# One table set for logarithm and exponential, evictions ahead of weight rounding on ScalarE, and a split order for the products of w2

## What is computed

```python
def first_block(x, p, ...):
    h = rms_norm(x, pre_norm_gain)
    q, k, v, z_a, b_gate, c_gate, u, z_c = split(h @ w_in, 8)      # 512 columns each
    attn = diff_attention(q, k, v, lam, slopes)                    # 4 heads, two softmaxes each
    attn = rms_norm(attn, subln_gain) * (1 - lambda_init) * silu(z_a)
    conv_out = b_gate * conv3(c_gate * u) * silu(z_c)
    x = x + rms_norm(concat(attn, conv_out) @ w_out, post_norm_gain)
    e = rms_norm(p @ w_ple_proj, ple_norm_gain)
    return x + sigmoid(x @ w_ple_gate) * e

def second_block(x, meta, ...):                                    # 16 meta tokens ahead
    n = rmsnorm(h, norm_mix)
    c_q, c_kv, k_pe, gq, gk, gv, ga, gg, gate_a, gate_b = split(n @ w_in)
    y_a = mla_branch(c_q, c_kv, k_pe, ...)                         # 8 heads, softmax
    y_b = gla_branch(gq, gk, gv, ga, gg, ...)                      # 4 heads with decay
    mix = sigmoid(gate_a) * (y_a @ w_o_mla) + sigmoid(gate_b) * (y_b @ w_o_gla)
    h = h + mix @ w_out
    h = h + peer_ffn(rmsnorm(h, norm_ffn), ...)                    # top 16 of 16384 experts
```

## Time and profile before

| | us |
|---|---|
| median of 3 runs | 2056.81 |
| lowest, highest | 2054.27, 2059.27 |
| the profiled execution | 2057.81 |
| its span, first to last instruction | 2056.0 |
| TensorE busy | 1908.5 |
| VectorE busy | 1288.2 |
| ScalarE busy | 1030.7 |
| GpSimd busy | 866.6 |
| mean granted clock of TensorE | 0.97 |

### The profile page before, as it was taken

How to read it: one execution, slowest core, us unless ns; L and a number is a source line. 1 busy time by engine, 2 the same in 40 slices (tenths; PEclk the granted TensorE clock), 3 DMA queues, 4 the chain that set the end, 5 groups by cost and what they waited for, 6 DMA issues and landing times.

```text
span 2056.0 us, 24907 instructions
## 1 busy us (share of the span) xinstructions
PE 1908.5 (93%) x9104; PEld 1484.3 (72%) x9104; DVE 1288.2 (63%) x2243; ACT 1030.7 (50%) x1656; POOL 866.6 (42%) x672
## 2 busy tenths in 40 slices
PE   7997989898978898998999989999998999999999
PEld 5775565467766666777777767777776888888887
DVE  6465374532336653468899968888863666656664
ACT  6465655744443426444444367777763433434341
POOL 5453452203122113775788789999983000000000
PEclk9999999999998899999999999999998999999999
DMA  6322223112111112442365547777679878888883
GB/s 223 116 103 103 103 92 98 43 31 92 42 62 42 42 41 82 143 161 90 98 225 196 187 160 236 264 273 284 255 263 373 301 281 296 286 287 294 283 297 138
DMA packets 98280, 359.15 MB, mean 175 GB/s; under 512 B 8480, under 2 KB 41504, under 8 KB 73328
## 3 DMA queue, kind: packets, MB, share of 16 engines
q1 hardware_dynamic: 98160, 357.56, 49.9%
HBM read 286.09 MB, written 71.30 MB: 174 GB/s over the span
## 4 chain that ended last, share of the span: by engine, by line
PE 55%; DVE 15%; POOL 14%; issue 7%; ACT 7%; DMA 2%; POOLq 0%; SPq 0%; ACTq 0%; DVEq 0%
PE ps L1434 11%; PE ps L1435 11%; PE ps L799 8%; PE ps L800 8%; POOL area L2651 6%; POOL wring_parts L2629 6%; PE ps L1245 3%; PE ps L788 2%; DVE area L2445 2%; ACT wring_parts L1479 2%; DVE area L2442 2%; PE ps L1221 1%; DVE area L2468 1%; PE ps L1382 1%; POOL wring_parts L2597 1%
## 5 line engine op out<-in xcount | busy, mean ns | idle before, releaser
L2597 POOL TENSOR_TENSOR wring_parts<-wring_parts,wring 128x512 fp32r<-128x512 f32 (+1 forms) x264 | 360.4, 1397 | 604.3 <-ACT wring_parts L1479 604.3
L1382 PE MATMUL ps<-sqbuf_parts,wring_parts 128*128 128x512 f32 x1024 | 410.3, 401 | 16.6 <-POOL wring_parts L2629 16.6
L1383 PE MATMUL ps<-normed_x_parts,wring_parts 128*128 128x512 f32 x1024 | 402.8, 393 | 0.0
L2629 POOL TENSOR_TENSOR wring_parts<-wring_parts,wring 128x512 fp32r<-128x512 f32 x256 | 328.3, 1314 | 66.8 <-ACT wring_parts L1884 63.8
L1382 PEld LDWEIGHTS ps<-sqbuf_parts,wring_parts 128*128 128x128 f32 x1024 | 194.7, 190 | 59.6 <-POOL wring_parts L2629 17.3
L800 PE MATMUL ps<-normed_x_parts,wring_parts 128*128 128x512 f32 (+1 forms) x624 | 235.5, 383 | 0.0
L1479 ACT ACTIVATE wring_parts<-wring 128x1024 fp32r<-128x1024 f32 (+1 forms) x132 | 125.3, 997 | 216.3 <-PE ps L800 181.3
L799 PE MATMUL ps<-resid_parts,wring_parts 128*128 128x512 f32 (+1 forms) x528 | 203.6, 393 | 26.3 <-issue 7.2
L1383 PEld LDWEIGHTS ps<-normed_x_parts,wring_parts 128*128 128x128 f32 x1024 | 194.7, 190 | 38.9
L1906 ACT ACTIVATE area<-ps 128x512 f32<-128x512 f32 x128 | 76.3, 597 | 195.1 <-PE ps L1383 195.1
L2531 DVE COPY area<-ps 128x512 f32<-128x512 f32 x128 | 138.8, 1086 | 54.2 <-PE ps L1409 54.2
(11 more groups left out here) (257 smaller groups left out, 3852.0 us busy)
## 6 DMA issues: line engine op xcount, KB each, us to landing
wring<-in_weights_dram SPq DMA_DIRECT2D x65, 1024.0 KB, 4.8
wring<-in_uT_dram SPq DMA_DIRECT2D x128, 512.0 KB, 4.3
area<-in_vT_dram SPq DMA_DIRECT2D x44, 1024.0 KB, 6.9
hidden_table<-area SPq DMA_DIRECT2D x32, 1024.0 KB, 6.5
gate_table<-area SPq DMA_DIRECT2D x32, 1024.0 KB, 8.1
area<-gate_table SPq DMA_DIRECT2D x32, 1024.0 KB, 9.1
wring<-in_vT_dram SPq DMA_DIRECT2D x20, 1024.0 KB, 7.2
rt<-hidden_table SPq DMA_DIRECT2D x32, 512.0 KB, 4.6
```

Source lines behind the costliest of these rows:

```text
L1382: pe.matmul(out, first[:, d], h_first[:, k, :], start=(k == 0), stop=False)
L1383: mm = pe.matmul(out, rest[:, d], h_rest[:, k, :], start=False, stop=(k == KD - 1))
L2597: ins = nc.gpsimd.tensor_tensor(rest[:, d, :], up[:, d, :], W(name)[:, d, :], ALU.subtract)
L2629: ins = nc.gpsimd.tensor_tensor(rest[:, a:a + PIECE], first[:, a:a + PIECE], u_raw[t % len(USLOT)][:, a:a + PIECE], ALU.subtract)
```

## The change

The table set that holds both Ln and Exp is loaded explicitly (`tables_for`), and explicit loads of the Silu, Sigmoid and Tanh sets stand ahead of the waits for the projections, with loads of the first set behind. ScalarE's order changes: q1's weights are rounded inside the rounding of h; in attention units `exps_a` and `exps_m` of u + 2 come ahead of the copy of the side projection, and `round_w` behind it; in a decay head the Tanh comes without `round_w` ahead, which moves to the end of the head; the four roots of the decay heads come ahead of the first Silu. On TensorE the products of w2 with inputs 6 and 7 are put behind others. On VectorE `scale_query(0)` moves from k == 6 to k == 3.

```diff
-            for m in range(4):
-                project_parts(("w2", m), MIX_PARTS, 3)
+            def mixed_out(m, a, ks):
+                key = ("w2", m)
+                if a == 0 and ks[0] == 0:
+                    claim(key)
+                up, low = split_arrived(f"w2{m}")
+                d = slice(a * P, (a + 1) * P)
+                for k in ks:
+                    if m == 0 and a == 0 and k % 2 == 0:
+                        pe.wait_ge(pair_split, 12 + k // 2 + 1)
+                    mm = two(pair(key)[:, a, :], (up[:, k, d], low[:, k, d]),
+                             (MIX_PARTS[0][:, k, :], MIX_PARTS[1][:, k, :]), k == 0, k == KD - 1)
+                if a == 1 and ks[-1] == KD - 1:
+                    fills(mm, key)
+            early, late = range(6), (6, 7)
+            for a in range(2):
+                mixed_out(0, a, early)
+            mixed_out(1, 0, early)
+            for a in range(2):
+                mixed_out(0, a, late)
+            mixed_out(1, 0, late)
+            mixed_out(1, 1, range(KD))
+            for m in (2, 3):
+                for a in range(2):
+                    mixed_out(m, a, range(KD))
...
+            def tables_for(name):
+                act.preload_act_table_set(name)
+            LOGS, SILUS, SIGMOIDS, TANHS = ("natural_log_exp_and_others", "silu_and_others", "sigmoid_and_others",
+                                            "exp_and_others")
...
+            tables_for(LOGS)
             for m in range(4):
                 act.wait_ge(x_first[m], 16)
...
-            round_h(0, "n1", T)
-            round_w(3)
+            round_h(0, "n1", T, {5: 3})
...
+                if u + 2 < len(UNITS_A):
+                    exps_a(u + 2)
                 if u in SIDE_A:
                     g, m = SIDE_A[u]
-                    round_w(SPLIT.index(f"{g}{m}") + NU)
+                    if g in ("zc", "za"):
+                        tables_for(SILUS)
...
-                if u + 2 < len(UNITS_A):
-                    exps_a(u + 2)
+                    round_w(SPLIT.index(f"{g}{m}") + NU)
+                    if g in ("zc", "za"):
+                        tables_for(LOGS)
...
             root("ple", T)
+            tables_for(SIGMOIDS)
             for m in range(4):
                 round_w(SPLIT.index(f"pg{m}") + NU)
                 copy_out(("pg", m), sgT[:, 2 * m:2 * m + 2, :], pair(("pg", m)), ACT.Sigmoid, scale=SCALE)
+                if m == 3:
+                    tables_for(LOGS)
...
+                if u + 2 < len(UNITS_M):
+                    exps_m(u + 2)
                 if u in SIDE_M:
...
                     elif g == "gk":
+                        copy_out(key, gk[:, m, :], flat(key)[:, MF], scale=SCALE)
                         round_w(SPLIT.index(f"gk{m}") + NU)
-                        copy_out(key, gk[:, m, :], flat(key)[:, MF], scale=SCALE)
...
                     if n == 3:
-                        round_w(SPLIT.index(f"ta{h}") + NU)
+                        tables_for(TANHS)
+                        when_filled(act, ("ta", h))
...
+                tables_for(LOGS)
                 if h + 1 < HG:
                     decay_terms(h + 1)
...
+                round_w(SPLIT.index(f"ta{h}") + NU)
             def square_head(h):
...
-            root("g0", T)
-            root("g1", T)
+            for h in range(HG):
+                root(f"g{h}", T)
+            tables_for(SILUS)
             silu(0)
-            root("g2", T)
-            root("g3", T)
...
+            tables_for(SIGMOIDS)
             sigmoid(0)
             for m in range(4):
                 round_w(SPLIT.index(f"ob{m}") + NU)
                 if m + 1 < 4:
                     sigmoid(m + 1)
+                else:
+                    tables_for(LOGS)
...
-                if k == 6:
+                if k == 3:
                     scale_query(0)
```

More of the change, by code:

```diff
@@ L1735, in copy_gv @@
                 else:
+                    copy_out(key, gvm[0:META, cols], flat(key)[0:META, 0:256], scale=SCALE)
                     round_w(SPLIT.index(f"gv{g}") + NU)
-                    copy_out(key, gvm[0:META, cols], flat(key)[0:META, 0:256], scale=SCALE)
             exps_m(0)
@@ L1752, in _ @@
                     if g == "gq":
+                        copy_out(key, gq[:, 2 * m + key[2], :], flat(key)[:, 0:T], scale=SCALE * HK ** -0.5)
                         if key[2]:
                             round_w(SPLIT.index(f"gq{m}") + NU)
-                        copy_out(key, gq[:, 2 * m + key[2], :], flat(key)[:, 0:T], scale=SCALE * HK ** -0.5)
                     elif g == "gk":
+                        copy_out(key, gk[:, m, :], flat(key)[:, MF], scale=SCALE)
                         round_w(SPLIT.index(f"gk{m}") + NU)
-                        copy_out(key, gk[:, m, :], flat(key)[:, MF], scale=SCALE)
                     else:
                         copy_gv(*key[1:])
-                if u + 2 < len(UNITS_M):
-                    exps_m(u + 2)
             copy_m(HM - 1)
```

## The result

The changed kernel takes 1990.39 us (median of 4 runs, 1986.6 to 1995.48) where the kernel before, run beside it, took 2056.29 us: a ratio of 0.968, with a 95% interval of 0.9655 to 0.9705. The forecast was 1991 us, with a range of 1974 to 2013. The profiled execution took 1989.75 us, with a span of 1988.0.

The account below looks back on a forecast made before the run. TensorE, busy 93% of the span, bounds the kernel, losing time to stalls and low clock. Terms up to the sort's beginning sum to -66.3 us, from 2057.8 to 1991.5, as a median 1991 us, range 1974 to 2013.

Parts of the forecast that it names:

- (b): Attention unit 0: second scores wait for q1's copy behind exponentials, a 5.2 us stall and low clock; net -0.5 with (a).
- (d): Attention unit 13: za0's Silu stands behind exponentials and a load; 3.2 us more stall, 0.7 for the clock: +3.9 us.
- (e): First block, chain from last tile over root to the 201.33 us stall: gains 2.6, loses 1.3; with clock, -3.0 us.
- Gates gg: New 1.8 us wait for gg2; gg3's split ready earlier (-3.9), low clock behind its wait gone (-2.8): together -6.7 us.
- w2: Products of w2: TensorE stalls 2.4 us for w21's split, later splits fit under VectorE's chain; -0.7 us (+1.1 to -1.9).
- The query's scaling: In ffn the 4.09 us wait ends earlier, but first scores' copy and sort stay behind pq3's rounding: 0 (-4 to +1).
- (a): First block: q1 rounded 3.6 us earlier; the 3.96 us stall at 46.44 and 2.3 us of low clock behind it go.
- (c): Attention unit 7: the Silu's load is done when the projection ends; with two shortened waits for VectorE, -2.4 us.
- (1): Rival, chance 0.12: half of the clock terms stays and levels of the decay heads wait for VectorE; 2004 us.
- (2): Rival, chance 0.06: late rounding puts GpSimd's splits in VectorE's way in the decay heads, costing 13 us; 2004 us.
- (3): Rival, chance 0.04: explicit loads don't keep automatic ones out; terms lose 13 us, 24 loads cost more; 2008 us.
- (5): Rival, chance 0.15: more gain, a far-end term in norms, w2 and ffn, first block's starts without low clock; 1976 us.

Follow-up runs that it names:

- The parts alone: The kernel before with one part of the change each: decay heads' reordering 2022.69 us, second attention's order 2047.73 us, explicit table loads 2032.76 us.
- the combined kernel: The changed kernel with copies first in units 0 and 13, logarithm load behind sl1's squares, early gg2 rounding, early w2 products cut to w20's halves: 1968.15 us.

## Why the prediction held, and where it did not

**The large terms** were right in cause and in size: heads 34.87 for 34.9, scores with the start of head 0 13.15 for 12.0, norms 5.27 for 5.0. The parts alone bear the causes out. The clock terms in the heads came in full.

**Units 0 and 13 (b, d)** went as worked out, a longer stall in exchange for a later copy; (d) cost 2.5 of 3.9 us. In (b) the stall was 4.19 us of the estimated 5.2, and of the 3.96 us at q1 1.96 stayed, so the net is 0 instead of -0.5. What the prediction did not say is that the trap was avoidable: it took the order as given and stopped at its price, while a few lines give 8.2 us back.

**The chain of sl1 (e)** gave 2.4 of 3.0. The failed step is "loses 1.3, since a load for the logarithm now stands ahead of the squares", counted as ScalarE's time alone. TensorE waits for these squares: its stall at their sum grew from 1.56 to 2.99 us, with a low clock behind it (0.64 over 8.4 us). TensorE then came so much later to the place of the 3.50 us stall (201.33 before) that no stall was left there.

**Gate and mix** gave 4.1 of 5.0. The stall of 3.27 us at 315.28 shrank to 1.44, nearly as forecast, but the waits of 1.26 and 0.34 us behind it, which the sum left out, became 0.37, 1.91 and 0.40.

**Gates gg** gave 4.4 of 6.7. Three sizes were off: the wait for gg2 was 2.66 us and not 1.8; it had a low clock behind it, for which the sum had nothing (0.90 over 16 us); and a wait of 1.00 us for the first sigmoid projection was missing. The step that all four roots in front are a gain was wrong in kind: with the first Silu between the roots and one table set for both functions, the stretch gave 7.5 us.

**w2** cost 1.15 us where -0.7 was forecast, at the bad end of the range given (+1.1). The wait for w21 was foreseen within 0.3 us (2.63 for 2.4). The failed step is "the later splits of w22, w23 fit under it": w22's did not, 2.67 us.

**The query's scaling** is the plain miss: 0 forecast, 4.02 us shown by the one line put back. The step "the sort with it" was true: the sort began at 886.54 instead of 950.08, 1.2 us of gain since the sums of ffn. Wrong was to take the sort for the finishing line. From there to the first expert tile TensorE's own queue sets the pace, with no wait over 0.5 us ahead of the tile's own, so what the 4.09 us of idle time and the low clock behind it had cost, less the new wait of 1.14 us, went straight through. The stretch from 1010 to 1200 us, on which I leaned, lies behind that tile and says nothing of what is in front of it.

**The sum** is better than its terms, and that is luck. Misses of 0.9 us in gate and mix, 2.3 in gg, 1.9 in w2 and 1.7 in (a, b), (c) and (e) together stand against 4.3 at the queries, 1.4 in (d), 1.2 at the scores and the 1.5 us of the last stretch. The prediction also passed over a group in its reading of the waits: 14.3 us for GpSimd's splits lie between the Tanh's 20.8 and the exponentials' 10.1. That group is 16.7 us in ten waits now. Though the 5.97 us of gg3 are gone, four waits of 2.66, 1.00, 2.63 and 2.67 us have come, just short of the 10 us that the prediction named as a sign of being wrong. Of the rivals, (1) and (2) did not come about ((2) was shown to be real once the rounding and its split are put behind the Tanh), (3) fell, and of (5) only the ffn part came.

**Open.** Why the low clock follows one stall of 2.6 us and not another is not settled. The spread of the expert stage was not looked into; its shortest and longest time, 1043.4 and 1054.3 us, come from one chip. Six of the experiments (all but the three parts, the loads taken out and the combined kernel) rest on one run each.

## What to carry to other kernels

On an engine that serves several others in order, put first what someone waits for now, and last what waits for a transfer or is used two stages on; then go through every place at which the new order puts a longer item ahead of a short one that is awaited, and make an exception there. Work that is pulled into a wait must have its own inputs ready and must not shorten the next piece that covers a split. A load of a function table belongs where its engine idles: behind the last instruction that others wait for, not ahead of it. And for each edit ask which engine's queue sets the pace up to the next fixed point, by its waits in that very stretch.

## What the runs showed of the hardware

Stalls of one length are not always followed by the same clock. Here are 16 us behind the wait of gg2, in the changed kernel (2.66 us of wait) and in the one with the old order of w2 (2.64 us):

```profile
744.14:760.14 16.00, 16.00 (x63) 12.96 (x64) 7.93 (x4) 5.17 (x6) 12.55 (x8) 0.90 0.29 103
```

```profile
746.82:762.82 16.00, 15.00 (x64) 11.94 (x65) 8.08 (x4) 6.08 (x7) 13.83 (x8) 1.00 0.29 106
```

The same 64 matmuls are done 1.4 us earlier in the second. Stalls of 1.59 and 1.32 us had the full clock behind them, one of 2.99 and one of 4.19 a low one (0.64 and 0.55 in the stretches above). In these traces a clock term for a stall between 2 and 3 us is thus a chance and not a sum. The other surprise is how far traces lie apart where the kernels' code is the same: up to 8 us by 690 us, and 11 us in the expert stage. Nine executions of the kernel before, the same program on one chip, went from 2055.42 to 2067.03 us.
